# Handing tiles to the matmuls by halves and by single inner tiles, in a two-block transformer kernel

## What is computed

```
first block, layer l = 0, 1:
  p = x @ w_in                      # swa, rwkv, fox, dsa branches and gates
  y = sum over branches of sigmoid(gate) * (branch @ w_branch) @ w_out
  x = layer_norm(alpha * x + y)
  l = 0: y = (silu(x @ w1) * (x @ w3)) @ w2      # dense, 2816 wide
  l = 1: y = the best 2 of 8 experts, 1408 wide  # router = x @ router_w
  x = layer_norm(alpha * x + y)
second block, layer l = 0, 1:
  h = rms_norm(x) * (1 + scale_a) + shift_a      # scale, shift from c @ w_mod
  q, k, v = split(h @ w_in_2); moba and differential attention
  x = x + gate_a * (o @ w_out_2)
  h = rms_norm(x) * (1 + scale_f) + shift_f
  x = x + gate_f * ((silu(h @ w_gate) * (h @ w_up)) @ w_down)
```

## Time and profile before

| | |
|---|---|
| median of 3 runs | 2228.22 us (2228.03 to 2229.43) |
| profiled execution | 2229.54 us |
| its span, first to last instruction | 2227.8 us |
| TensorE matmul busy | 2095.4 us (94%) |
| VectorE busy | 884.1 us (40%) |
| ScalarE busy | 374.3 us (17%) |
| mean granted TensorE clock | 0.971 |
| HBM traffic | 418 MB read, 188 GB/s over the span |

### The profile page before, as it was taken

One profiled execution on the slowest core, in us unless ns is written; L12 is line 12 of the kernel. 1 busy time (PEld: TensorE's weight loads), 2 busy tenths in 40 slices (PEclk: granted clock), 3 DMA queues, 4 the chain that ended last, 5 costly groups with the idle time before them and its releaser, 6 DMA issues.

```text
span 2227.8 us, 37306 instructions
## 1 busy us (share of the span) xinstructions
PE 2095.4 (94%) x16128; PEld 1552.6 (70%) x16128; DVE 884.1 (40%) x1887; ACT 374.3 (17%) x891; POOL 86.6 (4%) x180
## 2 busy tenths in 40 slices
PE   8998999998999989997999999899999988999998
PEld 7786776877777877765653554387687667858886
DVE  1415425677725144242110000235568753454433
ACT  1312230000013122301010000133300012331000
POOL 3000000010000000020000000000001020000000
PEclk9999899999999998997999999999999999999999
DMA  8333234498563342426999999852568763332552
GB/s 254 103 104 126 78 140 151 169 303 284 189 174 104 98 142 77 142 79 221 348 315 376 346 334 348 291 170 93 182 220 288 255 201 115 102 114 95 170 170 95
DMA packets 333831, 421.43 MB, mean 189 GB/s; under 512 B 27222, under 2 KB 282148, under 8 KB 333668
## 3 DMA queue, kind: packets, MB, share of 16 engines
q1 hardware_dynamic: 312464, 352.96, 49.0%
q0 software_dynamic: 13408, 50.66, 6.8%
q10 hardware_dynamic: 7796, 15.43, 2.0%
HBM read 417.90 MB, written 1.05 MB: 188 GB/s over the span
## 4 chain that ended last, share of the span: by engine, by line
PE 79%; DMA 9%; DVE 6%; ACT 3%; issue 1%; ACTq 1%; SPq 0%; DVEq 0%; POOL 0%
PE psum L1266 15%; PE psum L1298 11%; PE psum L1402 10%; PE psum L1273 9%; PE psum L1283 6%; PE psum L1462 5%; DMA ring<-in_ffn_w 3%; PE psum L1919 3%; DMA ring<-in_w_up 3%; PE psum L1532 2%; PE psum L1703 2%; PE psum L1310 2%; PE psum L1730 1%; DMA arena<-in_w_mod 1%; PE psum L1391 1%
## 5 line engine op out<-in xcount | busy, mean ns | idle before, releaser
L1266 PE MATMUL psum<-xT,ring 128*128 128x256 f32 x1600 | 369.3, 391 | 3.9 <-ACT small L775 2.1
L1266 PEld LDWEIGHTS psum<-xT,ring 128*128 128x128 f32 x1600 | 309.4, 196 | 58.6 <-issue 7.5
L1283 PE MATMUL psum<-ring,arena 128*128 128x512 f32 x528 | 232.6, 593 | 2.2 <-DVE arena L2157 2.2
L1273 PE MATMUL psum<-ring,xT 128*128 128x256 f32 (+2 forms) x960 | 206.1, 374 | 11.8 <-DVE arena L2383 4.4
L1273 PEld LDWEIGHTS psum<-ring,xT 128*128 128x128 f32 x960 | 174.8, 194 | 40.3 <-DVE arena L2383 5.7
L1283 PEld LDWEIGHTS psum<-ring,arena 128*128 128x128 f32 x528 | 97.7, 190 | 114.7 <-issue 113.8
L2091 DVE SCALAR_TENSOR_TENSOR arena<-arena,cond 128x256 f32<-128x256 f32 x336 | 137.4, 479 | 0.6
L1298 PEld LDWEIGHTS psum<-xT,ring 128*128 128x128 f32 x960 | 115.8, 198 | 24.3 <-issue 24.3
L1402 PE MATMUL psum<-ring,arena 128*32 128x256 f32 x2304 | 126.9, 379 | 0.7 <-DVE arena L2227 0.7
L1298 PE MATMUL psum<-xT,ring 128*128 128x128 f32 x960 | 116.5, 281 | 10.8 <-DMA ring<-in_w_up 5.4
L1298 PE MATMUL psum<-oT,arena 128*128 128x128 f32 x960 | 119.1, 278 | 7.0 <-DVE arena L2107 6.9
(11 more groups left out here) (415 smaller groups left out, 2510.4 us busy)
## 6 DMA issues: line engine op xcount, KB each, us to landing
ring<-in_w_in SPq DMA_DIRECT2D x80, 1024.0 KB, 5.3
ring<-in_exp_w SPq DMA_DIRECT2D x312, 256.0 KB, 5.9
arena<-in_w_mod POOLq DMA_DIRECT2D x48, 1024.0 KB, 10.2
ring<-in_ffn_w SPq DMA_DIRECT2D x33, 1024.0 KB, 7.6
arena<-in_exp_w SPq DMA_DIRECT2D x120, 256.0 KB, 7.1
ring<-in_w_gate SPq DMA_DIRECT2D x22, 1024.0 KB, 8.8
ring<-in_w_up SPq DMA_DIRECT2D x22, 1024.0 KB, 11.2
ring<-in_w_down SPq DMA_DIRECT2D x22, 1024.0 KB, 5.0
```

The lines of the kernel that those rows point to most:

```text
L1266: ins = pe.matmul(dst, w[:, k * 256 + c0:k * 256 + c0 + m], act_t[:, k, :], start=(k == 0), stop=(k == KT - 1))
L1273: ins = pe.matmul(dst, act_t[:, k, t * P:t * P + P], w[:, k * 256 + c0:k * 256 + c0 + n], start=(k == 0), stop=(k == KT - 1))
L1283: ins = pe.matmul(psum[:, 4 + 2 * t + h, :], gT[:, s % 2, f * 256 + t * P:f * 256 + t * P + P], w2[:, f * D + h * 512:f * D + h * 512 + 51 ...
```

## The change

The turning of a tile signals after each half (k = 3 and k = 7). ACT copies each half of a copied tile when that half is there, and TensorE waits for the first copy before inner tile 0 and for the second before inner tile 4. Of a modulated tile DVE starts after the first half and ACT after the second, each signals every inner tile, and TensorE takes the inner tiles in the order 0, 4, 1, 5, 2, 6, 3, 7 with a wait before each, in the first accumulation over the tile alone. Both modulated tiles are turned into banks 2 and 3, two banks away from where the matmuls write, and the modulation's columns of layer 1 move from bank 3 to bank 1.

```diff
@@ ACT @@
-                act.wait_ge(*ready("pe_job", "xt", *tag, t))
                 for j in range(2):
+                    act.wait_ge(*ready("pe_job", "xt", *tag, t, j))
                     step(act.copy(xT[:, 4 * j:4 * j + 4, t * P:t * P + P],
-                                  psum[:, 2 * t + j, :].rearrange("p (a b) -> p a b", a=4)), "xt", *tag, t)
+                                  psum[:, 2 * t + j, :].rearrange("p (a b) -> p a b", a=4)), "xt", *tag, t, j)
...
-                act.wait_ge(*ready("pe_job", "xt", which, l, t))
+                act.wait_ge(*ready("pe_job", "xt", which, l, t, 1))
                 for k in range(4, KT):
-                    step(act.activation(xT[:, k, t * P:t * P + P], psum[:, 2 * t + 1, (k - 4) * P:(k - 4) * P + P],
+                    step(act.activation(xT[:, k, t * P:t * P + P], psum[:, 3, (k - 4) * P:(k - 4) * P + P],
...
-                                        bias=modcol[:, l, 24 * i + k:24 * i + k + 1]), "modulated", which, l, t)
+                                        bias=modcol[:, l, 24 * i + k:24 * i + k + 1]), "modulated", which, l, t, k)
@@ TensorE: turn, turn_scaled @@
-                job(ins, "xt", *tag, t)
+                    if k % 4 == 3:
+                        job(ins, "xt", *tag, t, k // 4)
...
-                    ins = pe.matmul(psum[:, 2 * t + k // 4, (k % 4) * P:(k % 4) * P + P],
+                    ins = pe.matmul(psum[:, 2 + k // 4, (k % 4) * P:(k % 4) * P + P],
                                     x[:, t, k * P:k * P + P], diag[:, t, :], start=True, stop=True)
-                job(ins, "xt", which, l, t)
+                    if k % 4 == 3:
+                        job(ins, "xt", which, l, t, k // 4)
+
+            def copied(tag, t):
+
+                def wait(k):
+                    if k % 4 == 0:
+                        pe.wait_ge(*ready("act", "xt", *tag, t, k // 4))
+                return range(KT), wait
 
             def modulated(which, l, t):
-                pe.wait_ge(*ready("dve", "modulated", which, l, t))
-                pe.wait_ge(*ready("act", "modulated", which, l, t))
+
+                def wait(k):
+                    pe.wait_ge(*ready("dve" if k < 4 else "act", "modulated", which, l, t, k))
+                return (0, 4, 1, 5, 2, 6, 3, 7), wait
+
+            def arrived(order, wait, n):
+
+                for k in order:
+                    if n == 0:
+                        wait(k)
+                    yield k
@@ TensorE: first_step, token_tile, b1, f1, mix, ffn @@
-                    hand_over(t)
+                    order, wait = hand_over(t)
                     for i in range(2):
                         for f in range(2):
-                            for k in range(KT):
+                            for k in arrived(order, wait, i + f):
...
-                    pe.wait_ge(*ready("act", "xt", "b1", l, t))
+                    order, wait = copied(("b1", l), t)
...
-                            for k in range(KT):
+                            for k in arrived(order, wait, n + j):
...
-                    turn_mod(1, 3)
+                    turn_mod(1, 1)
...
-                    modulated("mix", l, t)
+                    order, wait = modulated("mix", l, t)
...
-                        ins = token_tile(psum[:, n, t * 256:t * 256 + 256], first[n], 0, 256, t)
+                        ins = token_tile(psum[:, n, t * 256:t * 256 + 256], first[n], 0, 256, t, arrived(order, wait, n))
@@ DVE: token_sums, modulate, mod_columns @@
-                dve.wait_ge(*ready("pe_job", "xt", which, l, t))
+                dve.wait_ge(*ready("pe_job", "xt", which, l, t, 0))
                 for k in range(4):
-                    free(dve.tensor_scalar(xT[:, k, t * P:t * P + P], psum[:, 2 * t, k * P:k * P + P],
+                    free(dve.tensor_scalar(xT[:, k, t * P:t * P + P], psum[:, 2, k * P:k * P + P],
...
-                    mod_columns(1, 3)
+                    mod_columns(1, 1)
```

More of the change, by code:

```diff
@@ L1268, in channel_tile, with token_tile @@
                 return ins
-            def token_tile(dst, w, c0, n, t, act_t=xT):
-                for k in range(KT):
-                    ins = pe.matmul(dst, act_t[:, k, t * P:t * P + P], w[:, k * 256 + c0:k * 256 + c0 + n],
+            def token_tile(dst, w, c0, n, t, order=range(KT)):
+                for k in order:
+                    ins = pe.matmul(dst, xT[:, k, t * P:t * P + P], w[:, k * 256 + c0:k * 256 + c0 + n],
                                     start=(k == 0), stop=(k == KT - 1))
@@ L1925, in normalised @@
                     turn(x, ("f1", l), t, ("ln", "ln1", l))
-                    pe.wait_ge(*ready("act", "xt", "f1", l, t))
+                    return copied(("f1", l), t)
                 if l == 0:
@@ L1931, in _ @@
                     for t in range(NT):
-                        normalised(t)
-                        for k in range(KT):
+                        order, wait = normalised(t)
+                        for k in arrived(order, wait, 0):
                             ins = pe.matmul(psum[:, 4, t * 8:t * 8 + 8], xT[:, k, t * P:t * P + P], router[:, k, :],
@@ L2028, in gated @@
                     turn_scaled("ffn", l, t)
-                    modulated("ffn", l, t)
+                    return modulated("ffn", l, t)
                 dense(("ffn2", l), gated)
@@ L2113, in token_sums @@
                 if key[0] == "ffn1":
-                    dve.wait_ge(*ready("act", "xt", "f1", 0, 1))
+                    dve.wait_ge(*ready("act", "xt", "f1", 0, 1, 1))
                 else:
-                    dve.wait_ge(*ready("act", "modulated", "ffn", key[1], 1))
-                    dve.wait_ge(*ready("dve", "modulated", "ffn", key[1], 1))
+                    dve.wait_ge(*ready("act", "modulated", "ffn", key[1], 1, KT - 1))
+                    dve.wait_ge(*ready("dve", "modulated", "ffn", key[1], 1, 3))
                 step(dve.tensor_tensor(xsum[:, 0], x12, x11, ALU.subtract))
@@ L2642, in modulate @@
                 i = 0 if which == "mix" else 1
-                dve.wait_ge(*ready("pe_job", "xt", which, l, t))
+                dve.wait_ge(*ready("pe_job", "xt", which, l, t, 0))
                 for k in range(4):
-                    free(dve.tensor_scalar(xT[:, k, t * P:t * P + P], psum[:, 2 * t, k * P:k * P + P],
+                    free(dve.tensor_scalar(xT[:, k, t * P:t * P + P], psum[:, 2, k * P:k * P + P],
                                            modcol[:, l, 8 + 24 * i + k:9 + 24 * i + k],
-                                           modcol[:, l, 24 * i + k:24 * i + k + 1], ALU.mult, ALU.add), "modulated", which, l, t)
+                                           modcol[:, l, 24 * i + k:24 * i + k + 1], ALU.mult, ALU.add), "modulated", which, l, t, k)
             for l in range(DEPTH):
```

## The result

| | before | after |
|---|---|---|
| first comparison, median (runs) | 2228.14 us (4) | 2206.46 us (4) |
| ratio, 95% interval | | 0.9906, 0.9892 to 0.9921 |
| all runs with their clock on record, mean (runs) | 2226.3 us (79) | 2207.0 us (10) |
| their mean granted TensorE clock | 0.9729 | 0.9750 |
| profiled execution, its span | 2229.54, 2227.8 us | 2209.55, 2207.8 us |

Of the drop, 20.0 us is seen between the two profiled executions, against 14.8 forecast. The first four runs of before have a mean of 2228.4, 2.1 above the mean of the 79 later ones, whose four sessions have means of 2226.2 to 2226.5. One execution of before, of 12183 us, is left out everywhere.

What follows compares the result with a forecast made beforehand. TensorE's 16 handover stalls, 23.7 us, bounded the gain. Places summed to 14.1, plus 0.7 for the clock: 14.8, so 2214.7 for the profiled execution and 2213.4 for the median, range 2207.5 to 2220.5.

Steps and rivals of the forecast that it cites:

- Copied handover, 0.92: At each copied tile (b1, f1), TensorE restarts 1.28 us after turning begins instead of 2.20, saving 0.92.
- Modulated handover, 1.27 and 1.48: At each modulated tile (mix, ffn), earlier inner tiles save 1.27 us with 128 columns or 1.48 with 256.
- b1, layer 0: Copied tiles of b1, layer 0: tile 0 wins 0.07 us before weights land, tile 1's 0.9 is lost; sum 0.1.
- b1, layer 1: Copied tiles of b1, layer 1: tile 0, in a low-clock stretch, wins 1.0 us, tile 1 wins 0.9.
- mix, layer 0: Modulated tiles of mix, layer 0: tile 0 wins 0.4 us before late weights, tile 1 passes 0.6 of 1.48.
- mix, layer 1: Modulated tiles of mix, layer 1: tile 0, turned at the low clock, wins 1.44 us, tile 1 1.48; sum 2.9.
- The other edits, 0: Bank moves, extra semaphore increments and 56 more TensorE waits, most satisfied when reached, were taken to cost 0.
- rival 1: Each of 56 added TensorE waits holds back the next weight load, 0.36 us each: 5.4 slower, 2233.6; chance 0.05.
- rival 2: Dense-layer transfers behind f1 and ffn of layer 0 land unchanged, low clock stays: 9.8 us left, 2218.4; chance 0.15.
- The clock, +0.7: Shorter low-clock stretches at mix, layer 0, and b1, layer 1, were together taken to add 0.7 us.
- rival 3: Both low-clock stretches shorten fully, 17.0 us, and a later one shrinks by another 1 to 2: 2210; chance 0.12.
- This profiled execution lies 1.3 above the median: The profiled run of before was 1.3 us above the runs' median, 2228.22, so the median forecast became 2213.4.

Runs made afterwards that it cites:

- experiment 7: The changed kernel with TensorE waiting before the inner tiles in every accumulation over a handed-over tile, 164 more waits: 2206.23 us, ratio 0.9914 to before.

## Why the prediction missed, by its own steps

**Copied handover, 0.92.** Right: 2.20 became 1.28 (385.31, 386.59), and TensorE's idle time 0.24.

**Modulated handover, 1.27 and 1.48.** Right: 1.33 at 128 columns; at 256, mix of layer 1, tile 1, from turning to the next stage 1859.04 - 1848.37 = 10.67 became 1842.60 - 1833.47 = 9.13, 1.54 (before, then after).

```profile
1848.37 1.95 PE L1199 MATMUL psum<-arena,x 128*128 128x128 f32 x16
1859.04 3.60 PE L1231 MATMUL psum<-arena,ones 128*128 128x512 f32 x8
```
```profile
1833.47 1.95 PE L1200 MATMUL psum<-arena,x 128*128 128x128 f32 x16
1835.25 0.60 PE L1291 MATMUL psum<-ring,xT 128*128 128x256 f32 x2
1836.02 6.74 PE L1291 MATMUL psum<-ring,xT 128*128 128x256 f32 x30 [0.17 <-ACT xT L985]
1842.60 2.74 PE L1249 MATMUL psum<-arena,ones 128*128 128x512 f32 x6
```

**Place by place** (forecast, then the profile):
- b1, layer 0: 0.1; 0.5. Tile 0 stayed at the weights (7.42). I held that ACT's second copy, and so the parameter loads behind it, came no earlier, and that tile 1's 0.92 was lost. That was wrong: ACT issued the first parameter load at 17.87 instead of 18.43, and the wait for the last fell from 0.86 to 0.54. But a little farther on TensorE then waited 0.52 for ACT (L779), which it hadn't before, so that from the turning of tile 1 to the products of 72 columns 52.27 - 17.35 = 34.92 became 51.24 - 16.79 = 34.45 (rows below). Over the profiles this stretch takes 34.56 to 34.92 in the seven with the old handover here and 33.64 to 34.79 in the nine with the new one, in the mean 0.4 less; where the parameters came early enough the whole 0.92 passed (33.64).
- f1, layer 0: 1.8; 2 x 0.92 = 1.8.
- b1, layer 1: 1.0 + 0.9; restarts 0.84 + 0.93, and the 64 rows in the low stretch 9.01 instead of 10.05, 1.0 more from the clock.
- f1, layer 1: 1.3; 1005.86 - 1002.73 = 3.13 became 996.75 - 994.96 = 1.79, 1.3.
- mix, layer 0: 0.4 + 0.6; 0.7 + 0.7. The weights are late next, as said, and the rows of tile 0 take 7.17 instead of 8.86, so that fall of the clock stayed away.
- mix, layer 1: 1.44 + 1.48; 1.6 + 1.5 by restarts. But behind tile 0's the clock stayed low and its 32 rows took 8.39 instead of 7.14, which gave 1.25 back.
- ffn: 5.1; 4 x 1.33 = 5.3.

The rows of b1, layer 0, before and after:

```profile
17.35 1.04 PE L1189 MATMUL psum<-ident,x 128*128 128x128 f32 x8
52.27 3.69 PE L1273 MATMUL psum<-ring,xT 128*128 128x72 f32 x32
```
```profile
16.79 1.04 PE L1189 MATMUL psum<-ident,x 128*128 128x128 f32 x8
46.74 0.43 PE L1765 MATMUL psum<-ident,arena 124*128 124x124 f32 x2 [0.54 <-DMA pos<-in_positions]
47.68 3.72 PE L1284 MATMUL psum<-xT,ring 128*128 128x256 f32 x16 [0.52 <-ACT arena L779]
51.24 3.69 PE L1291 MATMUL psum<-ring,xT 128*128 128x72 f32 x32
```

Sum 0.5 + 1.8 + 1.8 + 1.3 + 1.4 + 3.1 + 5.3 = 15.2, against 14.1 forecast and 15.4 +- 0.4 timed at equal clock. The handovers were sized right within 1.3; the largest pieces of that are b1 and mix of layer 0, 0.4 each.

**The other edits, 0.** Right for the waits: experiment 7 gives 0.002 us for one; rival 1 needed 0.26. The banks were never changed alone; 15.2 by rows and 15.4 by time leave next to nothing for them. Slack farther on (rival 2) ate nothing: by rows the copied part is worth 5.4 and the modulated 9.8, and 5.9 and 10.6 arrive at the end.

**The clock, +0.7: the step that failed.** I looked for the clock at two handovers only and let its gains and losses nearly cancel. The mean clock rose from 0.9729 to 0.9750, worth 0.0021 / 0.001 x 1.88 = 4.0 us. Adding TensorE's busy time times (1 - granted clock) over stretches of 1 us, the two profiled executions lose 51.9 and 47.5, 4.4 of their 20.0, and 15.6 is left; the second profiles lose 48.9 and 43.5. Of the 15.6, 0.6 lies in the first 64 rows of all (10.14 before, 9.53 after), where the profile lists a clock of 1.00, and 15.0 in the rest. So rival 3, at 0.12, is closest to what happened. Of the two stretches that it named, the one at b1 of layer 1 gave 1.0 and the one at mix of layer 0 its 1.7 in the profile, while mix of layer 1 took 1.25 back; the rest came at places that neither it nor the forecast looked at.

The section "What's actually happening" of the Trainium skill's page "TensorE: Matmul & The Clock Gate", by which low is the default and activity releases it, pointed the right way for the mean. The stretch at 859 doesn't follow from it as I read it: PE is busy 11.00 of 11.00 us there and the clock is 0.53. The work there is in part matmuls of 4 rows, in which PE counts as busy; that these bring the clock down is not shown.

**The sample.** "This profiled execution lies 1.3 above the median" was right for the three runs shown and wrong for the kernel: over 79 runs its profiled time lies 3.2 above the mean. The measured -21.7 of the first comparison is -19.4 over all runs; 15.4 of handovers, 4.0 of clock. The mean of after, 2207.0, lies 6.4 below my 2213.4, which is about the sum of 3.3 for the clock (4.0 less 0.7), 1.9 for the level of before and 1.3 for the handovers. Since 2206.5 misses the range by 1.0, any one of the three put right would have held it; the clock is the largest.

**Open.** Why the clock rose: one copied place alone does nothing, two raise it by 0.0013, three by 0.0024, and neither arrival alone nor the need for all three explains every run. The stretches that are shorter (624, 859, 999) are not the same ones in each profile, and one or two profiles of a kernel can't say more. A finer split of a copied tile, by quarters, wasn't tried: ACT would read a bank while TensorE writes to it.

## What to carry to other kernels

Where an engine waits for a whole tile that another hands over, hand it over by the pieces in which it is made, and let the consumer take them in the order of arrival: a satisfied wait inside an accumulation cost TensorE nothing measurable, and a handover gave 0.7 to 1.6 us that reached the end, except where something else was late (weights, parameters, the next tile's rows): there it gave little or nothing. Take first what is there first for longest: alternating between an early and a late producer left a stall of 0.39, and the order 0, 1, 2, 4 won 0.30 of it. And before a difference of some microseconds is explained, look at the spread of the granted clock over many runs of both kernels: three close times of one kernel were no measure of it.

## What the hardware showed that I had not expected

- The same program on the same chip took 2218.8 to 2234.1 us, at mean granted clocks of 0.977 and 0.971; 1.88 us for each 0.001.
- The granted clock can be at its lower level (1.2 GHz) while TensorE is never idle: 11.00 of 11.00 us busy at a mean clock of 0.53 (859 to 870, above). It covered matmuls of 64 and 4 rows and the dense ones behind them in one profile, and dense ones alone in another of the same program.
- 164 more satisfied waits in the middle of accumulations: 0.4 +- 1.0 us in all.
